# The first norm of a float32 two-block network on one core: X loaded ahead of the conditioning weights, sixteen conditioning columns computed as rows on four column tiles, second weight tile two k-tiles behind

## The reference, cut to what matters

```python
silu_c, silu_cc = silu(c), silu(c_ctx)              # one vector of 1024 each
mod_x = split(silu_c  @ ada_w[0] + ada_b[0], 6)     # latent tokens
mod_c = split(silu_cc @ ada_w[0] + ada_b[0], 6)     # context tokens
hx = rms_norm(x,   norm1_g[0]) * (1 + mod_x[1]) + mod_x[0]
hc = rms_norm(s_c, norm1_g[0]) * (1 + mod_c[1]) + mod_c[0]
y_c, y_x = hybrid_mixer(hc, hx, hyb_w_in, ...)      # its first step: [hc; hx] @ hyb_w_in
```

## Time and profile before

| what | value |
|---|---|
| median of three runs | 2632.99 |
| lowest and highest run | 2630.11, 2633.46 |
| span of the profiled execution, first to last instruction | 2627.3 |
| PE busy in it | 2563.2 (98%) |
| DVE, ACT busy | 1632.6 (62%), 964.2 (37%) |
| moved by DMA | 303.66 MB, 116 GB/s on average |
| mean granted TensorE clock | 0.989 |

### The profile page before, as it was taken

The page is one execution under the profiler, slowest core; times in us unless marked ns, Lnnn a source line. Parts: engine busy times, 40 slices in busy tenths (PEclk is TensorE's granted clock), DMA queues, the critical chain, the costliest instruction groups (busy, mean ns, idle before and its releaser), DMA issues.

```text
span 2627.3 us, 36055 instructions
## 1 busy us (share of the span) xinstructions
PE 2563.2 (98%) x13872; PEld 2124.3 (81%) x13872; DVE 1632.6 (62%) x2569; ACT 964.2 (37%) x1425; POOL 95.9 (4%) x185
## 2 busy tenths in 40 slices
PE   7999999999999999999999999999999999999998
PEld 4888888888888886669888887888888788888886
DVE  6777556654546556656555566675656876644446
ACT  4333533131313245764332243353232454532224
POOL 0000000000000000000000000000000000000000
PEclk9999999999999999999999999999999999999999
DMA  6432213433333321002544553234445422222222
GB/s 260 139 107 95 99 60 128 161 113 112 112 104 129 103 67 47 1 9 95 179 152 161 174 176 108 83 119 153 156 155 193 144 101 81 81 93 92 96 96 88
DMA packets 82937, 303.66 MB, mean 116 GB/s; under 512 B 9200, under 2 KB 11376, under 8 KB 81520
## 3 DMA queue, kind: packets, MB, share of 16 engines
q1 hardware_dynamic: 56736, 206.82, 23.1%
q0 software_dynamic: 26064, 94.91, 10.7%
HBM read 299.60 MB, written 2.10 MB: 115 GB/s over the span
## 4 chain that ended last, share of the span: by engine, by line
PE 93%; DVE 4%; ACT 1%; issue 1%; DMA 1%; SPq 0%; DVEq 0%; ACTq 0%
PE G L494 20%; PE G L496 20%; PE G L495 20%; PE G L521 5%; PE G L522 5%; PE G L523 5%; PE B L1024 2%; PE G L580 1%; PE G L582 1%; PE G L581 1%; PE G L986 1%; PE B L1000 1%; DVE Wlo L1712 1%; PE G L667 1%; PE G L669 1%
## 5 line engine op out<-in xcount | busy, mean ns | idle before, releaser
L1140 ACT ACTIVATE Whi<-Wraw 128x1024 fp32r<-128x1024 f32 x357 | 374.9, 1051 | 463.6 <-DMA Wraw<-wstream_dram 456.4
L1712 DVE TENSOR_TENSOR Wlo<-Wraw,Whi 128x1024 fp32r<-128x1024 f32 x357 | 436.4, 1222 | 128.0 <-ACT Whi L1140 126.8
L494 PE MATMUL G<-h_hi,Whi 128*128 128x512 f32 (+1 forms) x1024 | 361.0, 353 | 0.3 <-ACT T L1239 0.3
L496 PE MATMUL G<-h_hi,Wlo 128*128 128x512 f32 (+1 forms) x1024 | 358.7, 350 | 0.0
L495 PE MATMUL G<-h_lo,Whi 128*128 128x512 f32 (+1 forms) x1024 | 358.3, 350 | 0.0
L494 PE MATMUL G<-hs_hi,Whi 128*128 128x512 f32 x720 | 287.3, 399 | 4.1 <-DVE Wlo L1712 4.1
L496 PE MATMUL G<-hs_hi,Wlo 128*128 128x512 f32 x720 | 284.4, 395 | 0.0
L495 PE MATMUL G<-hs_lo,Whi 128*128 128x512 f32 x720 | 284.4, 395 | 0.0
L496 PE MATMUL G<-hid_hi,Wlo 128*128 128x512 f32 (+1 forms) x760 | 280.0, 368 | 0.0
L494 PE MATMUL G<-hid_hi,Whi 128*128 128x512 f32 (+1 forms) x760 | 279.9, 368 | 0.0
L495 PE MATMUL G<-hid_lo,Whi 128*128 128x512 f32 (+1 forms) x760 | 279.7, 368 | 0.0
(11 more groups left out here) (484 smaller groups left out, 4588.5 us busy)
## 6 DMA issues: line engine op xcount, KB each, us to landing
Wraw<-wstream_dram SPq DMA_DIRECT2D x357, 512.0 KB, 3.3
Araw<-adaw_dram POOLq DMA_DIRECT2D x180, 512.0 KB, 4.1
FIRST<-firstw_dram SPq DMA_DIRECT2D x6, 1024.0 KB, 21.8
X<-xin_dram SPq DMA_DIRECT2D x4, 1536.0 KB, 11.2
out_dram<-X SPq DMA_DIRECT2D x16, 128.0 KB, 1.7
ROW<-rows_dram SPq DMA_DIRECT2D x2, 768.0 KB, 7.6
CB<-cvec_dram SPq DMA_DIRECT2D x2, 512.0 KB, 10.8
CB<-cvec_dram POOLq DMA_DIRECT2D x1, 512.0 KB, 4.8
```

The source lines that it names most:

```text
L494: pe.matmul(o, wh, hi[:, a:b], start=(k == 0), stop=False)
L496: last = pe.matmul(o, wl, hi[:, a:b], start=False, stop=(k == kt - 1))
L1140: act.activation(Whi[:, t % 4, :], Wraw[:, t % 4, :], ACT.Copy).then_inc(w_hi, 1)
L1712: dve.tensor_tensor(Wlo[:, t % 4, :], Wraw[:, t % 4, :], Whi[:, t % 4, :].bitcast(F32), ALU.subtract).then_inc(w_lo, 1)
```

## The change

What it does, in the order of the engines:

- X comes first, in four pieces of two k-tiles each; then eight pieces of 1 MB of conditioning weights, piece i holding blocks i and i + 8, so that one piece has shift and scale of k-tile i. Piece 0 goes to Araw, piece 1 to CB, the others to FIRST. CON, and the first two weight tiles, lie between pieces. CB's own vectors are loaded after row 1, and Araw's first blocks after that.
- All sixteen blocks are computed on PE. The two columns are repeated 16 times (REP, 32 columns for each k-tile). A matmul of k-tile k goes to column tile k % 4, so output partitions 32 c to 32 c + 31, and each column tile sums two k-tiles. ACT copies 128 x 256 to SBUF in one piece, and a matmul with a matrix of ones and zeros (`pick_row`) sums the four column tiles and gives the columns.
- ACT makes gain and shift of a k-tile straight from those columns (`condition`), one k-tile at a time.
- The reciprocal root is copied from B4 to RS in SBUF (`keep_rstd`), since rows 2 to 7 use B4.
- The silu of the full vectors moves behind `first_upper` 5 and 6 on ACT and to the loop's tile 0 on DVE. Four `ada` blocks go away.
- Tile 1 of `first_products` is two k-tiles behind instead of three, and row n + 3 lies between the two products of step n, column n + 2 ahead of them.

```diff
-N_FIRST = 12
+N_FIRST = 16
...
+            for v in range(4):
+                sp.dma_start(X[:, 2 * v:2 * v + 2, :], xin[:, 2 * v:2 * v + 2, :]).then_inc(x_in[v], 16)
             first(0)
-            first(1)
-            for v in range(2):
-                sp.dma_start(CB[:, v, :], cvec[v]).then_inc(c_in, 16)
-            for v in range(2):
-                sp.dma_start(X[:, 4 * v:4 * v + 4, :], xin[:, 4 * v:4 * v + 4, :]).then_inc(x_in[v], 16)
             sp.dma_start(CON[:, :], consts_d).then_inc(const_in, 16)
-            for i in range(2, N_FIRST // 2):
-                first(i)
...
+            load(At(0))
+            first(1)
+            first(2)
+            load(At(1))
+            for i in range(3, KD):
+                first(i)
+            sp.wait_ge(row_done, 2)
+            for v in range(2):
+                sp.dma_start(CB[:, v, :], cvec[v]).then_inc(c_in, 16)
+            for u in range(2, N_HYB + 3):
                 load(At(u))
...
+            pool.wait_ge(row_done, 1)
+            pool.wait_ge(c_in, 32)
...
+            def first_row(i):
+
                 pe.wait_ge(first_in[i], 16)
+                wait(pe, row_kept, i)
+                if i == 2:
+                    pe.wait_ge(rstd_kept, 2)
+                for j in range(2):
+                    for c in range(4):
+                        k = 4 * j + c
+                        last = pe.matmul(mod_row(i)[32 * c:32 * (c + 1), :], REP[:, k, :],
+                                         piece(i)[:, :, k * P:(k + 1) * P], start=(j == 0), stop=(j == 1))
                 last.then_inc(row_done, 1)
...
+            pe.wait_ge(rep_ready, 1)
+            first_row(0)
             first_stats()
+            first_column(0)
             first_spread()
+            first_row(1)
+            first_column(1)
+            first_row(2)
+            first_column(2)
+
+            def early_row(n):
+
+                if n + 3 < KD:
+                    first_row(n + 3)
+
+            def early_column(n):
+
+                if 0 < n < KD - 2:
+                    first_column(n + 2)
+
             src = tiles(h0)
-            first_products(At(0), src, FULL, src_ready, At(8 * S_N0))
+            first_products(At(0), src, FULL, src_ready, At(8 * S_N0), between=early_column, middle=early_row, lag=2)
...
             def keep_row(i):
 
                 act.wait_ge(row_done, i + 1)
+                wait(act, mod_cols, i - 1)
+                act.activation(KEPT[:, i % 2, :], mod_row(i), ACT.Copy).then_inc(row_kept, 1)
+
+            def condition(k):
+
+                act.wait_ge(mod_cols, k + 1)
...
+                act.activation(GAIN[:, 0, 0, :, k], mod_col(k)[:, 2:4], ACT.Identity, scale=VEC[:, g:g + 1],
+                               bias=more_gain[:, k:k + 1]).then_inc(gain_ready, 1)
+                act.activation(MOD[:, 0, :, k], mod_col(k)[:, 0:2], ACT.Identity,
+                               bias=VEC[:, b:b + 1]).then_inc(shift_ready, 1)
...
+            for k in range(KD):
+                if k % 2 == 0:
+                    act.wait_ge(x_in[k // 2], 16)
+                first_square(k)
             keep_row(0)
...
+            first_deviation()
+            act.wait_ge(rep_ready, 2)
+            condition(0)
+            split_hi(At(0))
+            keep_rstd()
+            first_upper(0)
             keep_row(1)
+            condition(1)
             keep_row(2)
             first_upper(1)
             split_hi(At(1))
+            for k in range(2, KD):
+                keep_row(k + 1) if k + 1 < KD else None
+                condition(k)
                 first_upper(k)
+                if k in (5, 6):
+                    first_silu(k - 5)
...
             def first_shift(k):
 
+                dve.wait_ge(gain_ready, k + 1)
...
             dve.wait_ge(spread_done, 1)
             first_shift(0)
+            split_lo(At(0))
             first_lower(0)
+            dve.wait_ge(rstd_kept, 2)
+            for k in range(1, KD):
+                first_shift(k)
+                if k > 1:
+                    first_lower(k - 1)
+                if k == 2:
+                    split_lo(At(1))
+            first_lower(KD - 1)
...
+                if t == 0:
+                    silu_rows()
+                for _ in range(2 if t in (5, 6, 7, 8) else 0 if t in (0, 4) else 1):
```

More of the change, by code:

```diff
@@ L133, in build @@
         RCOL = small[:, 32:56]
+        one, pick_row = small[:, 55:56], small[:, 52:54]
+        more_gain = MRAW[:, 0, 0, 0:KD]
         ident = CON[:, C_ID:C_ID + P]
@@ L169, in build @@
         pr.close()
+        pf = ExitStack()
+        KEPT = sb("KEPT", [P, 2, 2 * P], where=pf)
+        REP = sb("REP", [P, KD, 32], where=pf)
+        pf.close()
         QS = sb("QS", [P, 2, NT], where=hyb)
@@ L260, in build @@
         const_in, c2_in = map(sem, ("const_in", "c2_in"))
-        x_in = [sem(f"x_in{i}") for i in range(2)]
+        x_in = [sem(f"x_in{i}") for i in range(4)]
         c_in, small_in, late_in, out_dma = map(sem, ("c_in", "small_in", "late_in", "out_dma"))
@@ L429, in stream @@
                     load(At(u))
-            for u in range(4):
-                load(At(u))
-            for u in range(4, N_HYB + 3):
+            load(At(0))
[8 more added lines that the diff above has]
+            for u in range(2, N_HYB + 3):
                 load(At(u))
@@ L506, in first_products @@
                     for e, nth in ((0, n), (1, n - lag)):
+                        if e == 1 and middle is not None:
+                            middle(n)
                         if not 0 <= nth < kt:
@@ L562, in first_stats @@
                 for c in range(TT):
-                    last = pe.matmul(B4[:, c:c + 1], RS[:, blk(c)], ones[:, 0:1], start=True, stop=True)
+                    last = pe.matmul(G[0][:, c:c + 1], RS[:, blk(c)], one, start=True, stop=True)
                 last.then_inc(col_done, 1)
@@ L2121, in _ @@
-            dve.wait_ge(silu_ready, 4)
-            def first_ada(n):
-                ada(At(N_FIRST + n), At(N_FIRST + n), 0, 2)
-            first_ada(0)
-            for k in range(3):
+            link(dve.tensor_tensor(small[:, 0:2 * KD], small[:, 16:16 + 2 * KD], vec("c", 0, 2 * KD), ALU.mult))
+            dve.tensor_copy(REP[:, :, :].rearrange("p k (r v) -> p k r v", v=2),
+                            small[:, 0:2 * KD].rearrange("p (k v) -> p k v", v=2).unsqueeze(2).broadcast_to(
+                                [P, KD, 16, 2])).then_inc(rep_ready, 1)
@@ L2128, in _ @@
+            dve.memset(one, 1.0)
+            dve.scalar_tensor_tensor(out=more_gain, in0=vec("ada_b", KD, KD), scalar=1.0, in1=vec("norm1_g", 0, KD),
+                                     op0=ALU.add, op1=ALU.mult).then_inc(rep_ready, 1)
+            for k in range(KD):
                 first_add(k)
-            first_ada(1)
-            for k in range(3, KD):
-                first_add(k)
-            first_ada(2)
+            dve.wait_ge(const_in, 16)
+            dve.tensor_reduce(pick_row, ident.rearrange("p (c r) -> p r c", c=4)[:, 0:2, :], AX.X,
+                              ALU.add).then_inc(pick_ready, 1)
```

147 lines of the change are left out of this document (50 added, 97 removed).

## The result

| | before | after |
|---|---|---|
| median of 7 runs each | 2631.26 | 2639.40 |
| lowest and highest | 2627.86, 2634.10 | 2635.43, 2645.19 |
| ratio, 95% interval | | 1.0035 [1.0023, 1.0046] |
| profiled execution: span, and its own time | 2627.3 | 2643.5, 2645.19 |
| first product | 49.45 | 29.73 |

The changed kernel is slower by 0.35%. The median lies inside my range, but on the other side of no change from my forecast. The profiled execution of after was the slowest of its seven, with a time 1.7 above its span. All the experiments' profiles show the same 1.7, so the profiled execution of before took about 2629, some 2 under its median of seven runs. The two profiles thus lie 16.2 apart where the medians lie 8.1 apart; the places of the loss can be read from them, their full size can't.

A forecast was written before the change was run, and what follows sets the result against it. PE, busy for 98%, was taken as the bound. First product 22.6 earlier, mostly given back in the loop: first two weight tiles end at 64.4 against 66.8, so 2633.0 - 2.4 = 2630.6, range 2623.5 to 2640.5.

The forecast's parts named there:

- The front: Path up to PE's first product: piece 0 at 13.3, spread until 20.3, first product at 26.8, 22.6 earlier.
- Four column tiles: A row's matmuls on PE: four tiles overlap, 0.87 plus 0.2 for the end at full clock.
- Rival 3: Column tiles on PE don't overlap beyond two (E 71.3, +4.5) or at all (E 86, +20); chance 0.10.
- The circle: Loop's chain of product, row, copy, gain, shift, lower: 5.15 a k-tile at full clock, 7.1 at low, five rounds.
- E: End of the first two weight tiles on PE: 66.80 before, forecast 64.4; what follows moves with it.
- The clock in the loop: PE's clock in the five rounds: first low, four high, rising near 30, 27.7 in all.
- Rival 2: PE's clock stays low through the loop: E 78.7, +12, time 2645; a rise at 46 gives 68; chance 0.10.
- the 3.6 between k-tiles 5 and 6: Loop's end: gain 7 waits behind upper 6 and one silu on ACT, so k-tile 6's product starts 3.6 later, 58.1.
- Behind E nothing: After the first two weight tiles: tile 0's emptying, DVE's silu, CB and POOL's blocks cost nothing, covered by PE.

The follow-up runs named there:

- The swap: The changed kernel with two lines exchanged on ACT, so gain k is made before row k+1 is copied: 2631.77, ratio 1.0006.
- The fillings: The changed kernel with matmuls that nothing reads added on PE, ahead of row 0 and in its gaps: 2627.57, ratio 0.9988.
- the repeat: The changed kernel run again with no edit: 2640.32, ratio 1.0033 to the kernel before.

## Why the prediction was wrong

**The front.** Forecast 26.8 for the first product, measured 29.7. The sum of squares was ready at 15.1 (14.3), piece 0 landed at 14.4 (13.3: the queues moved 407 GB/s from 5.0 to 14.4, not the 430 that I took), spread done at 22.6 (20.3), lower 0 at 26.3 (24.1). The largest miss is the sums over partitions: 2.72, where I had 1.5 and called them bound by weight loads, so not touched by the clock. They are touched: 1.50 at full clock, 2.72 at low. The picks are 0.50 at full clock (at 54.55) and 0.99 at low (at 18.83). Together with piece 0's lateness they make 2.9.

**Four column tiles.** I took 0.87 and 0.2 for the end, so 1.07 at full clock and 1.95 at low; measured 1.07 and 1.94. Rival 3 falls. From the Trainium skill's figure of 2.38 for three tiles ("TensorE: Matmul & The Clock Gate", Part 3, measured speedup) I had estimated 1.1 in place of the 0.87, so some 1.3 with the end. With the measured 3.64 on one tile the same efficiency gives 1.15, an estimate; the 1.07 of the trace is a little better than that.

**The circle.** Forecast 5.15 a round at full clock and 7.1 at low; measured 5.3 and 7.1, with copy 0.38, gain 0.35 (I had 0.22), shift and lower 1.15 and 1.14. The swap, which cuts only this circle, takes E from 73.9 to 59.8. This step was right.

**The clock in the loop: the step that failed.** I wrote "I take the first at low clock and four at high, the clock rising near 30". Three rounds were at low clock, the rise came at 49.5, and it fell again from 63.2 to 70.0, which doubled the last portions. That is 32.0 for the five rounds instead of 27.7, and 8.5 instead of 6.3 from k-tile 6 to E (the 3.6 between k-tiles 5 and 6 is as forecast). With the 2.9 of the front it makes the 9.5 between 64.4 and 73.9 (2.93 + 4.34 + 2.19, and 0.02 between k-tiles 5 and 6). Rival 2 was the right mechanism, in part of its length: it had 78.7 for a clock low throughout, and 68 for a rise at 46. The fillings show it by itself: same circle, same order, full clock from 25 on, rounds of 5.3, E 66.7. I had argued from the 3.5 of rows that lifted the clock in the kernel before. There they ran on without a gap; here PE stood still for a fifth of the time while the clock was low (busy 4.01 and 3.99 of 5.00 from 30 to 40). In which round the clock rises stays open beyond what the fillings show: seven profiles with PE's code equal up to E gave 73.8 to 74.0 five times, along two different paths of the clock, and 71.2 and 70.8.

**"Behind E nothing."** This is the second step that failed, a term put at nothing. Of the waits that I priced at nothing, none came: CB, POOL's blocks, the emptying of tile 0 and DVE's silu all stayed covered. What came was not in my list at all. PE's code ahead of the loop is longer, and with that the loop's second pass begins with a stop of 2.8 and, mostly, a stretch of low clock, some 5.5 in all by the table. That it depends on the length of the code ahead is shown, by adding instructions that do nothing: to before, which gets it, and to after, which loses it. It isn't the length as such: the stop comes back with exactly one block of 256 instructions more, and is absent at four other places within a block. That the period is 256 and no other number rests on this one pair, 115 and 371. The Trainium skill's rule of blocks of 256 ("Runtime: NRT & Kernel Launch", instruction fetch mechanics) agrees with that; its sentence that crossing from block to block is mostly hidden agrees with the long straight stretches here, which show no such waits without increments, and not with the loop's second pass. The packets say what the stop goes with: before runs the second pass without loading any instructions, after loads nine packets for it. A pass has 1579 instructions of PE in the trace, six blocks of 256 and 43 more; by an estimate from this it touches seven blocks from most places and eight from some 42 of the 256. If PE holds seven but not eight, one block too many makes it load the pass again. What PE holds was not measured, so this last step is argued.

**The sum.** The front gained 19.7, and the stretch from the first product to E grew from 17.35 to 44.15 by the circle and the low clock: E's +7.1. The stop adds about 5.5 in the profiles, and the medians show +8.1 (+10.0 in the repeat) where the two make 12.6. The difference of 2.6 to 4.5 is about what E and the tail scatter from one profile to another; it isn't explained further.

## What to carry to other kernels

When work on PE is spread out over a chain of other engines, price it at both clock levels and ask what PE did before, not how much it has to do. A chain that leaves it gaps of a microsecond in each round can go with half speed for much of the stage, as here up to 49.5; then the order of two small instructions on another engine, or matmuls that nobody reads, can be worth more than the microseconds that the change was to win (14.1 and 7.2 of E here, against a forecast of 2.4). And when PE's list of instructions ahead of a loop gets longer or shorter, look at the first instructions of the loop's second pass and at the number of instruction packets before reading a difference of 0.2% as the change's own; here 64 instructions of padding, where PE's queue runs ahead, took the stop away.

## What was unexpected of the hardware

- The stop: 2.3 to 2.9, once in a run of 2640, between two matmuls of one product, with the clock low for 3.4 to 6.8 from about its end in six profiles of eight. It was there at 115 and 371 instructions more than before, which are the same place modulo 256, and at none of 0, 179, 243, 274 and 530. With it the second pass of the loop was loaded again, nine packets, where the kernel before loaded nothing for 158.
- Padding isn't free everywhere. 159 increments ahead of row 0 moved it from 14.4 to 28.6 where PE could start on them from 4 on, about 0.15 each; 115 in before took 13.6, 0.12 each. Ahead of products in the steady state 8 a tile cost nothing that the profile shows, 13 a tile 3.3 in all, and 20 a tile 19.7.
- Matmuls of one column (sums over partitions) and of two (picks) slow down with the clock by 1.8 and 2.0 (2.72 against 1.50, 0.99 against 0.50), though their weight loads look like the bound.
- A trace whose first clock event is a rise prints 1.00 for all the time before it. The durations of a known shape are what to go by.
